# Mixture of experts: the fourth weight half of the next group is split at the end of the group before

## The reference

```python
hf = h.reshape(t, d)                              # 1024 x 1024
top_logits, top_idx = lax.top_k(logits, 4)        # of 32 experts
...
def expert_block(args):                           # the tokens of one expert
    xe, e = args
    gu = xe @ w_gate_up[e] + b_gate_up[e]         # 1024 -> 2048
    gate, up = jnp.split(gu, 2, axis=-1)
    gate = jnp.minimum(gate, 7.0)
    up = jnp.clip(up, -7.0, 7.0)
    act = gate * jax.nn.sigmoid(1.702 * gate) * (up + 1)
    return act @ w_down[e] + b_down[e]            # 1024 -> 1024
...
y_rows = yb.reshape(n_rows, d) * row_w[:, None]
return jnp.zeros_like(hf).at[row_tok].add(y_rows)
```

## Time and profile before

| | us |
|---|---|
| median of three runs | 2357.66 |
| lowest, highest | 2357.52, 2358.43 |
| the profiled execution | 2360.78 |
| its span | 2359.2 |
| TensorE matmuls busy in it | 2223.5 (94%) |
| VectorE busy | 1741.8 (74%) |
| ScalarE busy | 1291.3 (55%) |
| granted TensorE clock, mean share of full speed | 0.974 |

### The profile page before, as it was taken

One profiled execution on the slowest core, in us unless ns is written; L12 is line 12 of the kernel. 1 busy time (PEld: TensorE's weight loads), 2 busy tenths in 40 slices (PEclk: granted clock), 3 DMA queues, 4 the chain that ended last, 5 costly groups with the idle time before them and its releaser, 6 DMA issues.

```text
span 2359.2 us, 37522 instructions
## 1 busy us (share of the span) xinstructions
PE 2223.5 (94%) x10570; PEld 1817.7 (77%) x10571; DVE 1741.8 (74%) x2124; ACT 1291.3 (55%) x1736; POOL 791.9 (34%) x783
## 2 busy tenths in 40 slices
PE   6899997888975999999999999999999999999997
PEld 2679886776764888888888888888888888888886
DVE  1684422676765899977789977787999778799697
ACT  2332312675324677765567655566777656576575
POOL 2153103892125334332223322232333323243141
PEclk9899998899987999999999999999999999999998
DMA  7133204882235899987689967696999868799695
GB/s 244 67 125 144 67 18 120 251 238 73 108 125 170 291 379 379 375 308 226 225 287 373 372 230 236 228 327 233 383 379 367 310 221 289 257 331 383 230 364 170
DMA packets 299220, 583.98 MB, mean 248 GB/s; under 512 B 23889, under 2 KB 53601, under 8 KB 297057
## 3 DMA queue, kind: packets, MB, share of 16 engines
q1 hardware_dynamic: 269248, 501.68, 59.9%
q0 software_dynamic: 26560, 69.06, 10.5%
q10 hardware_dynamic: 3362, 12.59, 1.4%
HBM read 544.79 MB, written 44.24 MB: 250 GB/s over the span
## 4 chain that ended last, share of the span: by engine, by line
PE 63%; DVE 2%; issue 2%; ACT 1%; DMA 1%; DVEq 0%; POOL 0%; ACTq 0%; POOLq 0%; SPq 0%
PE psum L2036 56%; PE psum L2018 3%; PE psum L1976 2%; PE psum L1986 2%; DVE d_wlo L1863 1%; ACT d_whi L1739 1%; DMA d_raw<-in_w_down_dram 0%; DVE d_up L1876 0%; DVE d_act L1882 0%; DMA d_xg<-xn_d,d_entry 0%; DMA d_entry<-list_d 0%; ACT d_sg L1761 0%; DVEq L1542 0%; DVEq L1540 0%; DVEq L1541 0%
## 5 line engine op out<-in xcount | busy, mean ns | idle before, releaser
L1863 DVE TENSOR_TENSOR d_wlo<-d_raw,d_whi 128x1024 fp32r<-128x1024 f32 x578 | 674.0, 1219 | 74.8 <-ACT d_whi L1739 73.9
L1739 ACT ACTIVATE d_whi<-d_raw 128x1024 fp32r<-128x1024 f32 x578 | 573.6, 1053 | 112.1 <-PE psum L2036 79.7
L2036 PE MATMUL psum<-d_whi,d_xthi 128*128 128x512 f32 x1152 | 454.2, 394 | 0.2 <-issue 0.2
L2036 PE MATMUL psum<-d_whi,d_xtlo 128*128 128x512 f32 x1152 | 449.1, 390 | 0.0
L2036 PE MATMUL psum<-d_wlo,d_xthi 128*128 128x512 f32 x1152 | 449.0, 390 | 0.0
L1863 DVE TENSOR_TENSOR d_wlo<-slab,d_whi 128x1024 fp32r<-128x1024 f32 x292 | 343.6, 1219 | 15.5 <-ACT d_whi L1739 14.9
L1642 POOL DMA_INDIRECT out_dram<-d_yst,d_dest x49 | 94.3, 1925 | 750.9 <-DVE d_yst L1910 695.5
L1739 ACT ACTIVATE d_whi<-slab 128x1024 fp32r<-128x1024 f32 x292 | 291.8, 1054 | 4.8 <-PE psum L2036 4.4
L2036 PEld LDWEIGHTS psum<-d_whi,d_xthi 128*128 128x128 f32 x1152 | 216.6, 188 | 45.6 <-issue 2.1
L2036 PEld LDWEIGHTS psum<-d_whi,d_xtlo 128*128 128x128 f32 x1152 | 216.5, 188 | 45.7
L2036 PEld LDWEIGHTS psum<-d_wlo,d_xthi 128*128 128x128 f32 x1152 | 216.8, 188 | 43.2
(11 more groups left out here) (321 smaller groups left out, 4006.7 us busy)
## 6 DMA issues: line engine op xcount, KB each, us to landing
slab<-in_w_gate_up_dram SPq DMA_DIRECT2D x144, 1024.0 KB
d_raw<-in_w_gate_up_dram SPq DMA_DIRECT2D x144, 1024.0 KB, 8.4
d_raw<-in_w_down_dram SPq DMA_DIRECT2D x144, 1024.0 KB, 6.5
b_wp<-in_w_ada_dram POOLq DMA_DIRECT2D x16, 1024.0 KB, 6.6
slab<-in_w_in_dram SPq DMA_DIRECT2D x12, 1024.0 KB, 5.3
slab<-in_w_ada_dram SPq DMA_DIRECT2D x8, 1024.0 KB
a_xin<-in_x_dram ACTq DMA_DIRECT2D x2, 2048.0 KB
v_d<-a_vst POOLq DMA_DIRECT2D x16, 256.0 KB, 2.3
```

Source lines behind the costliest of these rows:

```text
L1739: nc.scalar.activation(whi[n % NW][:, part, :], raw[n % NRAW][:, part, :], ACT.Copy).then_inc(whi_ok, 1)
L1863: nc.vector.tensor_tensor(wlo[n % NW][:, part, :], raw[n % NRAW][:, part, :], whi[n % NW][:, part, :].bitcast(F32), ALU.subtract).then_inc ...
L2036: mm = nc.tensor.matmul(to, m_[:, KH * h + k, :], w_[n % NW][:, k, :], start=(h == 0 and k == 0 and q == 0), stop=(h == 1 and k == KH - 1 ...
```

## The change

The fourth weight half (n = 3) of the next group is no longer split at step 0 of that group but at the end of this one. On ScalarE its hi parts follow those of half 2 and stand ahead of the second block's `y_rows(g, 1)`. On VectorE its lo parts stand behind the first block's `output(g, 1, 0)` and ahead of the second block's `output(g, 1, 1)`. For the first group it is split ahead of the loops, and SyncE posts one more event for the group after the last, which no load fills.

```diff
@@ sync
-                for n in range(LEAD):
+                for n in range(LEAD + 1):
                     vacated(g, n)
                     sp.sem_inc(raw_in[n], 16)
@@ scalar, body
-                        if n + LEAD < NH:
+                        if n + LEAD >= NH:
+                            split(g + 1, n + LEAD - NH)
+                        elif n:
                             split(g, n + LEAD)
-                        else:
-                            split(g + 1, n + LEAD - NH)
+                    split(g + 1, LEAD)
                     if blocks == 2:
                         y_rows(g, 1)
@@ scalar, ahead of the loops
                 split(0, 2)
+                split(0, LEAD)
                 groups(act, body)
@@ vector, body
-                        if n + LEAD < NH:
+                        if n + LEAD >= NH:
+                            split(g + 1, n + LEAD - NH)
+                        elif n:
                             split(g, n + LEAD)
-                        else:
-                            split(g + 1, n + LEAD - NH)
-                    for b in range(blocks):
-                        output(g, 1, b, sh)
+                    output(g, 1, 0, sh)
+                    split(g + 1, LEAD)
+                    if blocks == 2:
+                        output(g, 1, 1, sh)
```

## The result

| us | before | after |
|---|---|---|
| median (lowest to highest) | 2358.05 (2357.52 to 2363.71), 6 runs | 2372.25 (2368.56 to 2373.53), 6 runs |
| profiled execution, span | 2360.78, 2359.2 | 2372.99, 2371.4 |
| granted TensorE clock | 0.974 | 0.974 |

The ratio is 1.0049, with a 95% interval from 1.0039 to 1.0060: by it the change costs about 11.6 us (9.2 to 14.1). The two medians of the table stand 14.2 apart, at that interval's upper end. The forecast was +11.3 us and 2369.0, with a range of 2359 to 2378.

The account below looks back on a forecast made before the run. The prediction took TensorE's own stream to bound the kernel, with loss only where TensorE waits. Terms of 3.1, 5.9 and 2.3 us summed to +11.3 us, from a median of 2357.7 to 2369.0, range 2359 to 2378.

Parts of the forecast that it names:

- Step 1: End of a two-block group before a one-block group: result and pick 1.71 us later, TensorE waits 1.71 us more.
- Step 2: Second turn of those seven one-block groups: 1.26 us won back, net loss 0.45 each, +3.1 us in all.
- Step 3: Five boundaries from two blocks to two: TensorE 1.18 us later each, nothing to win, +5.9 us.
- the signs: Marks expected in the after profile, such as pick waits of 1.7 us seven times and 0.7 five times.
- Step 4: Boundaries behind one-block groups: the pick moves to 880.8, in time for 881.2, so no cost; cover 0.4 us.
- Step 5: Program start: two lo parts ahead of group 0's pick cost +2.3 us, bounds 1.4 to 4.0.
- the last group: The moved steps fall behind the last group's result, beside its scatter, and cost 0.
- hidden behind the engine: Rival: VectorE's sequencer runs on, the pick directly follows the result, only the gain stays, -9 us; chance 0.08.
- The clock falls behind the new waits: Rival: TensorE's new waits lower its clock, +6.5 us more at about four places, 2375.5; chance 0.16.
- Late everywhere: Rival: the pick is late behind one-block groups too, about 1.5 us at some 13 boundaries, 2394; chance 0.05.
- The two effects cancel: Rival: sum and lo parts interleave better, half the delay and all the gain remain, about 2360; chance 0.09.

Follow-up runs that it names:

- e1: The changed kernel, but both engines deal with the second block's result before splitting the fourth half; 2365.55 us against 2359.77 for the kernel before, ratio 1.0022.
- e3: The kernel before with only ScalarE's hi parts moved, VectorE keeping its old order; 2368.46 us, ratio 1.0037 to the kernel before.
- e4: The kernel before plus, in VectorE's two-block body, a wait for its own last result and a 128x1 memset; 2365.14 us, ratio 1.0026.
- e5: The kernel before plus two subtractions of the moved kind on VectorE behind the loops; 2362.08 us, ratio 1.0006.
- e6: The kernel before with only the fourth half's first part moved to the group's end, between the two results; 2358.88 us against 2359.81, ratio 0.9995.
- e10: e6 with the bias product three products later in one-block groups and the bias's low part ahead of half 2 before the loops; 2356.71 us, ratio 0.9995.
- e2: The changed kernel with the fourth half's two parts on either side of the second block's result; 2361.67 us against 2359.77 for the kernel before, ratio 1.0008.
- e9: e2 with the bias product three products later in one-block groups and the bias's low part ahead of half 2 before the loops; 2354.78 us, ratio 0.9979 to before.

## Why the prediction was right, and the step that failed

- **Step 1, held.** The pick moved from 5.16 to 6.91 after the group's start, +1.75 where 1.71 was worked out, and TensorE waits 1.6 to 1.7 for it. The cause named there, a sequencer held at the wait ahead of the result with the branches and table loads behind it, is what e1, e3 and e4 show: 3.56 to 3.57 from the last wait to the pick, whatever VectorE runs meanwhile.
- **Step 2, held.** The wait at the second turn is gone. Net +0.43 for each of seven on average where 0.45 was forecast, 3.0 in all against 3.1. That the won 1.26 depends on the lo parts and not on the hi parts was not said there; e3 shows it.
- **Step 3, held in its way, a little small.** +1.29 for each of five where 1.18 was forecast, 6.5 against 5.9. Both waits are in the rows, shorter than the signs named them (0.57 for 0.7 at the pick, 0.19 for 0.4 behind it), yet the second block's first product came 6.96 after the group's start in place of 5.77, +1.19 as worked out. The other 0.1 arises later in the group.
- **Step 4, held.** One-block groups behind one-block groups last 35.9 as before; their pick in the outer loop comes at 4.6, for which 4.7 was worked out (880.8 - 876.14). The cover of 0.4 us was enough. In the inner loop the pick follows the lo parts at once, at 4.3 in place of 2.0, and is in time too.
- **Step 5, the wait held, the clock left open.** +2.66 where 2.3 was taken. The pick came 2.27 later after the group's start (10.55 for 8.28; its wait went from 1.85 to 4.13). The other 0.39 falls behind the bias product, where the clock stayed at the lower level for 4.98 us in place of 3.87. What a stretch costs can be read from kernels with the same start as before: before and e3 had one of 3.41 us around the pick, and their group 0 took 65.59 and 65.63; e4 and e5 had none and took 64.01 and 63.94. So a stretch costs 1.6 to 1.7, as was worked out. Against e4 and e5 the start costs 4.2 to 4.3, against before 2.66: how much is seen depends on the stretches that an execution happens to have. The forecast had this in its bounds (1.4 to 4.0), not in its 2.3.
- **The step that failed: the last group.** "It falls behind the last group's result [...] beside its scatter: 0." It was not 0 but 1.16 by the scatter, and 1.68 from the last matmul to the end. That the moved subtractions and the scatter run side by side was taken for free, without a row for it. The other 0.5 is no more than two kernels with an equal scatter differ by (e6 15.46, e10 14.94).

The sum was +11.3; the profiled executions give 9.28 + 2.66 + 1.68 = 13.6 for the parts that the change touches, less 1.42 of other stages. The ratio gives 11.6 and the medians 14.2 (2372.25, where 2369.0 was forecast). That the sum meets the ratio to 0.3 us is partly luck: the tail's 1.7 and steps 3 and 5 were each sized low, together by 2.6.

The rivals: *hidden behind the engine* is refuted by e4, where a wait with 0.06 us of work behind it moved the pick by 0.79. The Trainium skill's rule (Advanced Engine Details and Errata, Sequencer Loop) that an engine instruction is queued and the sequencer reads on does not fit an instruction that has yet to wait: in before the branch behind the result starts at 1203.84, when the sum has ended, and not when the sum has started (1203.11) and the result could have been queued behind it. It fits instructions whose waits had passed: in e1 and e2 the head's work did run under such lo parts. *The clock falls behind the new waits*: 1.00 from 752 us on; waits of 1.7 us left it there at all seven places. Only the first group's 4.13 stands beside longer time at the lower level. *Late everywhere*: no wait for the pick behind one-block groups. *The two effects cancel* did not happen in the change but does in e2 and e6 (2361.67 and 2358.88, neither to be told from the kernel before).

## What to carry to other kernels

On an engine with a loop, look at the last semaphore wait ahead of the branch back: whatever delays it delays the whole next head, and work that is already free to run costs nothing behind it (two lo parts of 2.35 us did not, under a head of 3.5). So moved work goes behind a wait that has already passed, in small parts (e2), not ahead of a wait that others depend on. And if something is then late by a fixed amount, the consumer may be moved too (e9), but only as far as needed: with six products (1.4 us) the other groups lost 4.5 us and the seven won 4.7, because 1.4 is more than VectorE's slack of about 1.2; three products, in one-block groups alone, stayed inside it and kept the 4.7. Before a saving is counted, undo the bottleneck that hides the next one: e6 and e2 looked alike until the bias product moved, and only e2 then won.

## What the runs showed of the hardware that was not expected

**A scatter that meets a row of subtractions is held up.** GpSimd's last scatter takes 1.67 us with VectorE idle (before) and 2.83 when it starts within two lo parts that follow each other without a gap (after, e5); a lo part subtracts with both inputs in SBUF. In after it starts at 2357.90, the row ends at 2359.19, and the scatter ends 1.54 after that. Whether the whole scatter or one phase of it is held up, the rows don't tell. All 49 scatters of the expert stage, before and then after (ns: least, median, most):

```profile
L1642 POOL DMA_INDIRECT out_dram<-d_yst,d_dest x49: 1434/1646/5323, 753.6 to 2347.4; - x49
```

```profile
L1642 POOL DMA_INDIRECT out_dram<-d_yst,d_dest x49: 1434/1661/2865, 751.8 to 2357.9; - x49
```

The medians hide it: in before five of the 49 take more than 2.4 us, in after 23 take 2.83 to 2.87. What tells them apart is what VectorE does as the scatter starts. None of the scatters that start while no lo part runs takes more than 1.67 us, in any of the twelve kernels, though many have one beside them later on. In after, the 23 long ones are just those that start within a lo part. A scatter that starts within a lo part ends some 1.5 us after that part, or after the row of parts that follow it without a gap: with 0.19 of a last lo part ahead of it it takes 1.72 (e2, e6), within four in a row 5.3 (before, four times; from 915.06, with the row's end at 918.85). Two of the six in before follow this less well: the one at 1351.76 (2.50) went by the first of two parts, and the one at 1414.87 took 1.60. Why was not tested. Mid-stage none of this costs anything: no wait of TensorE names GpSimd.

The Trainium skill has a mechanism that fits (SBUF — State Buffer, Who interferes with whom): VectorE's instructions with two SBUF inputs contend with GpSimd's instructions that read SBUF. The trace agrees, with 1.67 against 2.83, where the scatter starts within such an instruction; beside one that starts later it shows nothing.

**A loop's head costs 3.5 us on VectorE's sequencer**, three table loads and the branches of two nested loops. From the branch at 1203.84 to the pick at 1207.36 pass 3.52. On VectorE's timeline it shows only as "issue" ahead of the pick, 2.78 us, and it is hidden or not by what was queued before it.

Left open: which part of a scatter is held up, and what decides how many stretches at the lower clock the first group has.
